# Moving the weights' low-part buffer by 192 bytes in a two-block transformer kernel

## The reference, cut to what matters

```python
# first block (h: 272 x 2048)
h = h + hybrid_mixer(rmsnorm(h), ...)      # w_in 2048x6152: q, k, v, two gates, conv input, forget logits; w_out 2048x2048
h = h + (silu(h_ @ w_gate) * (h_ @ w_up)) @ w_down      # h_ = rmsnorm(h); inner width 5632
x = rmsnorm(h)[16:]
# second block (x: 256 x 2048)
h = x @ w_in_2                              # 2048x8192: q, k, v, pool input, two gates
x = layer_norm(ALPHA * x + (gated attention branch + gated pool branch) @ w_out_2)
f = square(relu(x @ w_ff1)) @ w_ff2         # inner width 8192
x = layer_norm(ALPHA * x + f)
```

## Time and profile before

| | |
|---|---|
| median of three runs | 2472.88 us |
| the profiled execution's own time | 2471.54 us |
| its span, first to last instruction | 2469.7 us |
| granted TensorE clock, mean share | 0.997 |
| TensorE busy with matmuls | 2439.0 us (99%), 14746 |
| TensorE busy with weight loads | 2172.6 us (88%), 14746 |
| VectorE busy | 1619.7 us (66%), 2471 |
| ScalarE busy | 1200.2 us (49%), 1729 |
| GpSimd busy | 214.7 us (9%), 231 |
| DMA | 449.60 MB, 182 GB/s |

### The profile page before, as it was taken

The page is one execution under the profiler, slowest core; times in us unless marked ns, Lnnn a source line. Parts: engine busy times, 40 slices in busy tenths (PEclk is TensorE's granted clock), DMA queues, the critical chain, the costliest instruction groups (busy, mean ns, idle before and its releaser), DMA issues.

```text
span 2469.7 us, 36384 instructions
## 1 busy us (share of the span) xinstructions
PE 2439.0 (99%) x14746; PEld 2172.6 (88%) x14746; DVE 1619.7 (66%) x2471; ACT 1200.2 (49%) x1729; POOL 214.7 (9%) x231
## 2 busy tenths in 40 slices
PE   8999999999999999999999999999999999999996
PEld 8898898888888888888888888888998888888886
DVE  5645676766666665667677756678785665565667
ACT  6444545544444443445555654544454443443544
POOL 0001111000000000002221112023200000000022
PEclk9999999999999999999999999999999999999998
DMA  7554456566666566665655456565466656666663
GB/s 247 179 155 127 129 171 189 190 189 185 196 188 192 183 196 190 191 187 190 196 185 169 167 181 195 186 191 178 151 198 190 191 188 189 192 190 191 183 195 103
DMA packets 125752, 449.60 MB, mean 182 GB/s; under 512 B 13840, under 2 KB 16400, under 8 KB 125584
## 3 DMA queue, kind: packets, MB, share of 16 engines
q1 hardware_dynamic: 125296, 446.91, 57.8%
q10 hardware_dynamic: 288, 0.36, 0.0%
HBM read 445.12 MB, written 2.10 MB: 181 GB/s over the span
## 4 chain that ended last, share of the span: by engine, by line
PE 96%; DVE 3%; ACT 1%; issue 0%; DMA 0%; ACTq 0%; POOL 0%; POOLq 0%; DVEq 0%
PE out_bank L599 27%; PE out_bank L603 27%; PE out_bank L600 14%; PE out_bank L602 14%; PE out_bank L606 3%; PE out_bank L607 3%; PE out_bank L608 3%; DVE w_lo L1224 1%; PE side_bank L678 0%; ACT w_hi L833 0%; PE side_bank L677 0%; PE side_bank L716 0%; DVE h L1600 0%; DVE b_op L1655 0%; PE side_bank L707 0%
## 5 line engine op out<-in xcount | busy, mean ns | idle before, releaser
L1224 DVE TENSOR_TENSOR w_lo<-raw,w_hi 128x1024 fp32r<-128x1024 f32 x839 | 1040.4, 1243 | 603.5 <-ACT w_hi L833 599.4
L833 ACT CAST w_hi<-raw 128x1024 fp32r<-128x1024 f32 x840 | 877.9, 1049 | 959.1 <-PE out_bank L603 876.1
L599 PE MATMUL out_bank<-a_op,w_hi 128*128 128x512 f32 x1984 | 784.6, 395 | 1.4 <-DVE h L1251 0.8
L603 PE MATMUL out_bank<-a_op,w_hi 128*128 128x512 f32 x1984 | 776.7, 391 | 0.0
L600 PE MATMUL out_bank<-a_op,w_lo 128*128 128x256 f32 x1984 | 558.9, 282 | 0.0
L602 PE MATMUL out_bank<-a_op,w_lo 128*128 128x256 f32 x1984 | 552.1, 278 | 0.0
L602 PEld LDWEIGHTS out_bank<-a_op,w_lo 128*128 128x128 f32 x1984 | 380.1, 192 | 84.4
L600 PEld LDWEIGHTS out_bank<-a_op,w_lo 128*128 128x128 f32 x1984 | 372.9, 188 | 76.9
L599 PE MATMUL out_bank<-b_op,w_hi 128*128 128x512 f32 x992 | 389.8, 393 | 0.0
L603 PE MATMUL out_bank<-b_op,w_hi 128*128 128x512 f32 x992 | 388.0, 391 | 0.0
L599 PEld LDWEIGHTS out_bank<-a_op,w_hi 128*128 128x128 f32 x1984 | 373.1, 188 | 4.2 <-DVE w_lo L1224 1.8
(11 more groups left out here) (285 smaller groups left out, 2006.3 us busy)
## 6 DMA issues: line engine op xcount, KB each, us to landing
raw<-in_w_ff SPq DMA_DIRECT2D x256, 512.0 KB, 4.3
raw<-in_w_in SPq DMA_DIRECT2D x223, 512.0 KB, 3.7
raw<-in_w_gu SPq DMA_DIRECT2D x176, 512.0 KB, 4.2
raw<-in_w_down SPq DMA_DIRECT2D x88, 512.0 KB, 4.2
raw<-in_w_out SPq DMA_DIRECT2D x64, 512.0 KB, 4.3
raw<-in_w_ba SPq DMA_DIRECT2D x16, 512.0 KB, 3.8
raw<-in_w_bp SPq DMA_DIRECT2D x16, 512.0 KB, 4.1
out<-h SPq DMA_DIRECT2D x8, 256.0 KB, 2.1
```

What stands on the lines that cost most here:

```text
L599: t_.e.matmul(bank[:, :], wh, a_both, start=start, stop=False, skip_group_check=True)
L603: mm = t_.e.matmul(bank[:, :], wh, a_both, start=False, stop=stop, skip_group_check=True)
L833: a.e.copy(w_hi[:, m % SPLIT, :], raw[:, u % RAW, :]).then_inc(hi_split)
L1224: v_.e.tensor_tensor(w_lo[:, m % SPLIT, :], raw[:, u % RAW, :], w_hi[:, m % SPLIT, :].bitcast(F32), ALU.subtract).then_inc(lo_split)
```

## The change

Two buffers are declared elsewhere. `tiny` (192 bytes) now stands ahead of `w_lo`, and `cq` (64 bytes) behind it. No instruction is added, removed or reordered.

```diff
         w_hi = sb("w_hi", [P, SPLIT, UNIT], F32R)
+        tiny = sb("tiny", [P, 3, 16])
         w_lo = sb("w_lo", [P, SPLIT, UNIT], F32R)
+        cq = sb("cq", [P, 2, HEADS])
         q = sb("q", [P, HEADS, SEQ])
...
         cneg = masks[H8, sum(KEYS1):sum(KEYS1) + TOK]
-        cq = sb("cq", [P, 2, HEADS])
         gms = sb("gms", [P, KT, 2])
         work = [sb(f"work{i}", [P, TOK]) for i in range(8)]
-        tiny = sb("tiny", [P, 3, 16])
         soft = sb("soft", [P, 2, 3, 2])
```

## The result

The changed kernel takes 2511.11 us (2509.14 to 2512.82, four runs) against 2473.14 us of the kernel before in the same comparison. The ratio is 1.0153 with a 95% interval of 1.0137 to 1.0169: slower by 38 us, where I had forecast no change and a range that ended at 2494.

What follows compares the result with a forecast made beforehand. TensorE's matmul spacing was taken to bound the kernel. All terms came to 0: 2471.54 + 0 = 2471.5 us, forecast as 2473 us on the median's scale, with a range of 2451 to 2494 for 8 times in 10.

Steps and rivals of the forecast that it cites:

- What bounds the kernel: TensorE, with a matmul in flight for 2439.0 of 2469.7 us: time is the number of matmuls times their spacing.
- the value taken for the group: Pair form's group of four matmuls, one every 0.694 us: moving w_lo was taken to change its spacing by nothing.
- the second of the three readings: Direct stage q, same weights at other streaming distances: four medians sum to 1344 ns against 1343 in later stages.
- the nearest row: Profile rows of the pair form itself, in direct stage q and later stages, taken as showing no change.
- the parities of L606: Direct stage k: L606 lasts 292 ns for even kt, 285 for odd, with only the streaming start changed, distance 0 to 128.
- The bounds: L599 and L600, about 4 ns each: 8 ns x 2976 = 24 us a group form, slower at worst, faster at best.
- Rival A: L599 and L600 of later groups: low-weight load runs into the stream, slower, 2485 or 2497 us; chance 0.33.
- its own marks: Profile signs for the slower case, between 500 and 560 us: L600 at 286 ns or more and L599 at 396.
- Rival B: L600, perhaps L599: low-weight load comes out of the stream's way, faster, 2461 or 2449 us; chance 0.30.
- Rival C: w_lo: an absolute phase of 192 would help but it gets 64; 2473 us, counted with no change, 0.37.
- The other terms: VectorE's write of w_lo, the moved gms and work buffers, tiny and cq: each counted at zero.
- The 4 ns for each slice of the three-matmul form: The 760 triples, each with one w_lo load: bounded at 4 ns x 760 = 3 us either way.

Runs made afterwards that it cites:

- e5: Kernel before with all buffers unmoved, the later stages' streaming operand rows starting at PLACE 0 instead of 48 floats; 2501.1 us.
- e6: Kernel before with w_hi moved by 192 bytes instead of w_lo (tiny ahead of w_hi, cq behind it); 2509.2 us.
- e3: Kernel before with both w_hi and w_lo moved by 192 bytes (tiny ahead of w_hi, cq behind w_lo); 2516.4 us.
- e13: Kernel before with 40 of 128 weight columns in the pair form's two low-weight matmuls, L600 and L602; 2507.7 us.
- e4: Kernel before with every large buffer moved by 192 bytes, streaming operands and both weight parts alike; 2473.6 us.
- e2: Kernel before with only gms and the eight work buffers moved by 192 bytes, w_lo unmoved; 2473.0 us.
- e7: Changed kernel with the main products loading w_hi's slice where they should load w_lo's; VectorE still makes w_lo; 2472.9 us.
- e11: Kernel before with the later stages' streaming rows at PLACE 32, distance 128 from both weight parts; 2517.7 us.
- e8: Kernel before with w_lo moved by 64 bytes (cq ahead of it, tiny behind); 2502.5 us.
- e16: Kernel before with the streaming rows at PLACE 56, 32 bytes later, distance 224 from both weight parts; 2516.1 us.
- e15: Kernel before with the streaming rows at PLACE 44, 16 bytes earlier, distance 176 from both weight parts; 2472.3 us.

## Why the prediction was wrong

**What bounds the kernel** was right: the time is the number of matmuls times their spacing, and the spacing is all that changed.

**The step that failed** is the value taken for the group, "nothing ... by the nearest row, the pair form itself". It rested on the second of the three readings, that in stage q the group's sum is unchanged (1344 against 1343) while its parts move by 2 to 4 ns: "what one matmul gains the next gives back". Those were sums of four medians of durations, and the medians of the earlier trace rows hid what the spread beside them shows: 388 to 483, 275 to 283. Groups of unlike length lie behind it. The starts of L599 in that stage of the kernel before, each a group later, ahead of a break at 71 us with other matmuls in it and behind it:

```profile
69.70 0.39 PE L599 MATMUL out_bank<-a_op,w_hi 128*128 128x512 f32 x1
...
70.39 0.39 PE L599 MATMUL out_bank<-a_op,w_hi 128*128 128x512 f32 x1
...
75.89 0.39 PE L599 MATMUL out_bank<-a_op,w_hi 128*128 128x512 f32 x1
...
76.58 0.40 PE L599 MATMUL out_bank<-a_op,w_hi 128*128 128x512 f32 x1
...
77.29 0.39 PE L599 MATMUL out_bank<-a_op,w_hi 128*128 128x512 f32 x1
...
77.98 0.40 PE L599 MATMUL out_bank<-a_op,w_hi 128*128 128x512 f32 x1
```

0.69 ahead of the break; 0.69, 0.71, 0.69 behind it, the group of 696 and that of 704 ns in turn, mean 700. Ahead of it groups take 693 to 694 ns, at the same phases: as in e5, one placement ran in two patterns. The twenty groups of the stage that nothing interrupts have a mean of 697.0 ns, 3.3 above the later stages, and 3.3 ns x 2848 is 9 us; by the slow part alone it would be 6.3 ns and 18 us. Nor are differences of durations those of the spacing to the nanosecond, as the prediction reads them: in e6 L602's record grew by 2 ns and its distance to the next start by 4.2. Read by its starts, then, the nearest row spoke for a loss, if not for one as large as the 14.1 ns that were measured. And it was less near than I took it for: in stage q both weight parts have one phase, and the change gives them two. No row of the kernel before showed that case. The rows that I set against the value, the parities of L606, pointed to the right side, but by a price on a load at distance 0, which the runs refute; that they did so is luck as much as evidence.

**The bounds were too narrow**, and that in the mechanism, not in a size. I had bounded the loss by giving 4 ns to each of two matmuls, those beside a load of `w_lo`, 8 ns a group. It was 14.1, and by the starts only 4.0 of it stood at L599 and L600, while 10.1 stood at L602 and L603, beside loads that hadn't moved. Rival A had the sign, and by its own marks it failed: L600 was to be at 286 or more and stayed at 282 (L599 was to be at 396 and is at 398). A price for each collision can't be right, since the mirror (e6) pays at the unmoved side, twice the collisions cost hardly more (e3), the same collisions go with the old speed for 220 us of e5, and shorter loads cost more (e13).

**Rival B** was wrong: L600's median stayed at 282 and the time rose. **Rival C** was wrong as an idea of absolute phase (e4), and right in that 64 is what `w_lo` gets. **The other terms**, VectorE's write, the `work` buffers, `tiny` and `cq`, were right at nothing: the intervals of e2 and e7 leave them 0.1% either way. The 4 ns for each slice of the three-matmul form (3 us) came out as about 1 us, towards faster.

The Trainium skill's "SBUF — State Buffer", section "Who interferes with whom", gives the two reads of TensorE independent ports. That can't be carried over to time in this kernel: e4, e5 and e11 show that the places of the two reads count against each other, by up to 1.8%. Whether the ports are the reason, they don't show.

**What is shown and what isn't.** Shown: the loss is `w_lo`'s place, through the loads, relative to the streaming operand, modulo 256 among the steps tried, and it takes the form of another repeating sequence of start distances: one group before, six in the changed kernel, two in e11, three in e8, nearly one but longer in e6 and e13. Shown as well: where one placement has several sequences (e3, e5, e16), it changes between them within an execution. Not shown: what in the chip these sequences follow, and what picks one. The cause below the level of addresses stays open. Nor did any place beat the old one: e15 is level with it (0.9987 to 1.0006), the others are slower.

## What to carry to other kernels

When one engine is busy 99% of the time with one short group of instructions, read the distances of starts over a dozen groups before you argue from medians: medians of durations hid here that groups of 696 and 704 ns took turns. That groups are all alike doesn't prove them fast, though: those of e6 and e13 are, at 706.5 ns. Only the comparison with another placement tells. Place the streaming operand and the buffers of the weights as one set, test a move of one against the others by the measured time, and move them together where something must move. In this kernel a buffer slipped in between two of them was free when it was 256 bytes, and cost 1.2 to 1.6% at 64, 128 and 192; with another size than a multiple of 256, time the whole set again.

## What the runs showed of the hardware that I had not expected

- A matmul's spacing at full granted clock depended on the place of its weights against its streaming operand: four matmuls with 1536 columns took 693.4 to 709.7 ns on average over ten pairs of distances.
- Two of the four matmuls with 40 weight columns in place of 128, loads included, made the group longer, 706.6 against 693.7 ns.
- One program can fall into unlike patterns within an execution, and its time can differ from one to the next. e5, with all its distances at 0, has stretches at 713.3, 693.3 (the old speed) and 700.0 ns in one trace, and e3's four runs were 2511.2, 2511.4, 2521.5 and 2521.5 us, while the kernel before kept within 2471.1 to 2474.8 in all its runs.
